# Casting the next weights between the exponential and the second table load, in the hybrid attention, RWKV-7 and PEER block

## The reference

```python
def peer_ffn(xn, peer_wq, peer_subkeys, peer_u, peer_v):
    ...
    best_s, best_pos = lax.top_k(cand_s, PEER_TOPK)
    idx = jnp.take_along_axis(cand_i, best_pos, axis=-1)
    gates = jax.nn.softmax(best_s, axis=-1)
    ...
        u_g = peer_u[ic]
        h = jax.nn.gelu(jnp.einsum('chkd,cd->chk', u_g, xc).astype(f32), approximate=False) * gc
        v_g = peer_v[ic]
        return jnp.einsum('chk,chkd->cd', h.astype(peer_v.dtype), v_g)
```

## Time and profile before

| | |
|---|---|
| Time, median of 3 runs | 948.08 us (948.0 to 948.29) |
| The profiled execution's own time | 948.34 us |
| Its span, first to last instruction | 946.3 us |
| TensorE busy, share of the span | 937.5 us, 99% |
| Chain that ended last | TensorE 98% |
| Granted TensorE clock | 0.998 |

### The profile page before, as it was taken

One profiled execution on the slowest core, in us unless ns is written; L12 is line 12 of the kernel. 1 busy time (PEld: TensorE's weight loads), 2 busy tenths in 40 slices (PEclk: granted clock), 3 DMA queues, 4 the chain that ended last, 5 costly groups with the idle time before them and its releaser, 6 DMA issues.

```text
span 946.3 us, 21227 instructions
## 1 busy us (share of the span) xinstructions
PE 937.5 (99%) x7136; PEld 903.5 (95%) x7136; DVE 756.3 (80%) x1645; ACT 623.8 (66%) x1231; POOL 645.9 (68%) x326
## 2 busy tenths in 40 slices
PE   9999999999999999999999999999999999999997
PEld 8998898898889999999999999999999999999996
DVE  7684674745755799888788888749999999999997
ACT  6874377655657567677899999865555555555554
POOL 4696635487425999999988889975655566567650
PEclk9999999999999999999999999999999999999999
DMA  7463312355654766666655556679999999999991
GB/s 268 146 235 133 134 49 94 126 183 181 223 195 137 247 218 219 219 220 212 196 184 181 183 202 225 220 262 409 409 390 390 393 388 378 403 392 377 400 356 45
DMA packets 67041, 232.32 MB, mean 246 GB/s; under 512 B 8211, under 2 KB 10259, under 8 KB 66860
## 3 DMA queue, kind: packets, MB, share of 16 engines
q1 hardware_dynamic: 52732, 180.78, 53.8%
q0 software_dynamic: 13824, 50.34, 14.0%
q10 hardware_dynamic: 432, 0.55, 0.2%
HBM read 229.67 MB, written 1.06 MB: 244 GB/s over the span
## 4 chain that ended last, share of the span: by engine, by line
PE 98%; DVE 1%; DMA 1%; ACT 0%; issue 0%; POOL 0%; DVEq 0%
PE PS L1008 21%; PE PS L1079 20%; PE PS L1012 12%; PE PS L1083 12%; PE PS L559 6%; PE PS L954 3%; PE PS L568 3%; PE PS L636 2%; PE PS L640 2%; PE PS L637 2%; PE PS L965 2%; PE PS L1033 1%; PE PS L1034 1%; PE PS L549 1%; PE PS L736 1%; PE PS L551 1%
## 5 line engine op out<-in xcount | busy, mean ns | idle before, releaser
L1649 POOL TENSOR_TENSOR lo<-raw,hi 128x1024 fp32r<-128x1024 f32 x191 | 457.6, 2416 | 130.5 <-ACT hi L1167 130.1
L1167 ACT CAST hi<-raw 128x1024 fp32r<-128x1024 f32 x202 | 211.5, 1048 | 56.3 <-DMA raw<-in_u_units 34.0
L1008 PE MATMUL PS<-xb,hi 128*128 128x416 f32 x1024 | 219.8, 356 | 0.0
L1079 PE MATMUL PS<-xb,hi 128*128 128x416 f32 x1008 | 213.2, 352 | 0.0
L1008 PEld LDWEIGHTS PS<-xb,hi 128*128 128x128 f32 x1024 | 182.6, 189 | 0.9
L1079 PEld LDWEIGHTS PS<-xb,hi 128*128 128x128 f32 x1008 | 179.2, 189 | 1.0
L2369 DVE TENSOR_TENSOR lo<-raw,hi 128x2048 fp32r<-128x2048 f32 x63 | 144.2, 2289 | 7.2 <-ACT hi L1526 7.0
L1526 ACT CAST hi<-raw 128x1024 fp32r<-128x1024 f32 x128 | 134.1, 1048 | 4.8 <-DMA raw<-in_v_units 4.8
L1012 PEld LDWEIGHTS PS<-xb,lo 128*128 128x128 f32 x1024 | 133.3, 191 | 1.8 <-POOL lo L1649 1.2
L1012 PE MATMUL PS<-xb,lo 128*128 128x208 f32 x1024 | 133.7, 273 | 0.0
L1083 PEld LDWEIGHTS PS<-xb,lo 128*128 128x128 f32 x1008 | 132.3, 191 | 1.2 <-DVE lo L2369 0.8
(11 more groups left out here) (391 smaller groups left out, 1510.5 us busy)
## 6 DMA issues: line engine op xcount, KB each, us to landing
raw<-in_u_units SPq DMA_DIRECT2D x128, 512.0 KB, 3.2
raw<-in_v_units SPq DMA_DIRECT2D x128, 512.0 KB, 6.7
raw<-in_w_in_units SPq DMA_DIRECT2D x43, 512.0 KB, 3.3
raw<-in_w_q_units SPq DMA_DIRECT2D x16, 512.0 KB, 3.4
raw<-in_w_proj_units SPq DMA_DIRECT2D x8, 512.0 KB, 3.3
raw<-in_w_out_units SPq DMA_DIRECT2D x8, 512.0 KB, 3.3
arena<-bias_rows SPq DMA_DIRECT2D x2, 512.0 KB, 5.7
arena<-in_subkeys_t SPq DMA_DIRECT2D x1, 1024.0 KB, 6.8
```

The lines of the kernel that those rows point to most:

```text
L1008: mm(o[:, 0:2 * TD], hi[:, w, P * k:P * k + P], joined[:, k, 0:2 * TD], start=(k == 0), stop=False, skip_group_check=True)
L1079: return mm(PS[:, V_BANKS[c], 0:2 * TD], hi[:, (U_V + j) % 4, P * c:P * c + P], coef_slot(u + j)[:, 0:2 * TD], start=start, stop=False, sk ...
L1167: nc.scalar.copy(hi[:, j, :], raw[:, j, :]).then_inc(hi_made, 1)
L1649: nc.gpsimd.tensor_tensor(lo[:, w, :], raw[:, w, :], hi[:, w, :].bitcast(F32), ALU.subtract).then_inc(lo_pool, 1)
```

## The change

ScalarE's rows for units 52 to 55 are put in another order. The cast for unit 56 (`hi_ahead(U_U, PICKS_AT, 2)`) stands between the exponential and the load of the gelu table, where it stood behind the right copy of unit 53. The gelu of unit 52 stands directly behind the right copy of unit 53, where it stood behind the right copy of unit 54. Nothing is added or removed.

```diff
             first_half_gelu(PICKS_AT, -1)
             act.wait_ge(shift_made, 2)
             nc.scalar.activation(bvs, bvs, ACT.Exp).then_inc(exp_made, 1)
+            hi_ahead(U_U, PICKS_AT, 2)
             nc.scalar.preload_act_table(ACT.Gelu)
             right_copy(PICKS_AT, 1)
-            for j in (2, 3):
-                hi_ahead(U_U, PICKS_AT, j)
-                right_copy(PICKS_AT, j)
-                first_half_gelu(PICKS_AT, j - 2)
+            first_half_gelu(PICKS_AT, 0)
+            right_copy(PICKS_AT, 2)
+            hi_ahead(U_U, PICKS_AT, 3)
+            right_copy(PICKS_AT, 3)
+            first_half_gelu(PICKS_AT, 1)
             with act.Fori(PICKS_AT + 1, FIRST // 4) as i:
```

## The result

The changed kernel takes 950.95 us (median of 20 runs, 948.08 to 955.94), the kernel before 948.68 us (20 runs, 947.45 to 951.27). The ratio is 1.0026 with a 95% interval from 1.0016 to 1.0035: 1.5 to 3.3 us slower. I had forecast 0.26 us less, and a range that ended at 948.6.

The account below looks back on a forecast made before the run. TensorE, with 98% of the chain that ended last, was taken as the bound. One term, −0.26 us, took the profiled 948.34 to 948.08; the median's 0.26 us lower level gave 947.82 us, range 947.3 to 948.6.

Parts of the forecast that it names:

- the one on the gelu of unit 52: ScalarE around the softmax: gelu runs 427.12 to 427.48 against 427.10 to 427.46 before, freeing unit 56's bank in time.
- the table load's move: ScalarE behind unit 56's cast: load ends at 426.76, right copy of unit 53 starts 1.08 us later, no net cost.
- a rule on table loads: Trainium skill's drain of about 1380 ns per ScalarE table switch; by it the sum was about 949.0 us.
- the gain: TensorE at unit 56's low products: wait for GpSimd's subtraction gone, 0.26 us saved, bounds 0.22 and 0.33.
- The cast starts at once: ScalarE, unit 56: cast at 424.41, right behind the exponential, 1.52 us earlier, weights landed 0.8 us ahead.
- the subtraction is ready for TensorE: GpSimd, unit 56: subtraction runs 425.54 to 427.93, wanted at 429.18, 1.2 us to spare.
- the cast of unit 57 is no bound: ScalarE, unit 57: cast 0.24 us later, subtraction done at 431.10, wanted at 431.60, half a microsecond of cover.
- The rival of the dearer table switch: ScalarE: table load waits for the cast to leave the engine, up to +0.83 us, 948.9 us; chance 0.05.
- The rival of the late weights: ScalarE: unit 56's weights land late, delaying cast, load and gelu of unit 52; up to +1.07 us, 949.15; chance 0.06.
- The rival of a gain that is lost again: TensorE: 0.26 us lost again at unit 57 or the next wait, L1083; 948.08 us; chance 0.17.

Follow-up runs that it names:

- the gelu alone: Kernel before with only the gelu of unit 52 moved ahead of the right copy of unit 54: 948.87 us, ratio 1.0002.
- the staging edit on before: Kernel before with row numbers staged ahead of the exponential, one operand in PSUM, and gates by a product with reciprocal sums in PSUM: 948.46 us, ratio 1.0005.
- both rows out of the way: Changed kernel with row numbers staged ahead of the exponential, one operand in PSUM, and gates by a product with reciprocal sums in PSUM: 948.3 us, ratio 1.0.

## Why the prediction was wrong

**The step that failed** is the one on the gelu of unit 52: "In the new order the gelu has only the copy of unit 53 ahead of it, and runs from about 427.12 to 427.48", and, of the table load's move, "Cost nothing; cover that small." I took VectorE's sum of unit 52 to start at 426.69 as before, because no VectorE row had moved. But what runs beside those rows had: my own sum moved a GpSimd subtraction to 425.54, on top of VectorE rows that had stood in GpSimd's idle time. The sum started at 428.43, and the gelu ran from 428.83. I looked at which engine waits for which semaphore, and this wait has none; it shows as the duration of a row.

The Trainium skill has the rule, on the page "SBUF — State Buffer", section "Who interferes with whom": a VectorE instruction with two inputs in SBUF contends with a GpSimd instruction that reads SBUF, copies can enter a mode that contends as well, and the one that issues second blocks until the first ends. The traces agree: 2.30, 2.44 and 2.37 us for the two-operand row against 0.29, 2.03 to 2.41 us for the copy against 0.22, and 0.29 with one operand in PSUM. In all of these GpSimd came first; no run here shows it waiting for VectorE. I had weighed a rule on table loads and missed the one that decided.

**The term that was mis-sized** is the gain: "I take the middle one, 0.26". The wait of 0.33 us for unit 56's subtraction was that one execution's. In two other profiles with the cast in its old place (the gelu alone, the staging edit on before) it is 0.07 and 0.06 us, and the chain has the low products of unit 56 at the usual 0.88 us there, so the term measures nothing. In the profile of before, unit 55's cast stood 5.76 us ahead of the transposes (421.37 to 427.13), in these two 6.01 and 6.03: the softmax and the cast behind it happened to be late by a quarter of a microsecond. Such a small wait can stand elsewhere, too: the kernel with both rows out of the way has one of 0.34 us ahead of unit 52's low products. That kernel is 0.36 us better than the profile of before in the stretch and not to be told from it in the runs.

**The range** stood on the spread of 0.3 us in three runs. Over 20 runs the kernel before goes from 947.45 to 951.27 us, and its median, 948.68, lies above the end of my range with no change at all; less 0.26 it would have been 948.42, near the end. So even a right sum would have been inside only just.

**What was right.** The cast starts at once, its weights having landed; the subtraction is ready for TensorE with time to spare; the cast of unit 57 is no bound. The rival of the dearer table switch falls: the load follows the cast after 0.02 us (424.06 + 1.03 = 425.09, 425.11), lasts 1.28 us, and the copy starts 0.01 us behind it. The drain that the Trainium skill adds to each switch (the page "ScalarE: Activation LUTs", section "What ACT_TABLE_LOAD costs") is not to be seen there either. The rival of the late weights falls too: no wait for a load stands ahead of that cast. Both rivals had the place right, the bank of unit 52, and prices, 1.07 and 0.83 us, near the 1.2 us that the stretch of the first profile grew by. That is luck, for neither had the mechanism, and neither allowed for more. The rival of a gain that is lost again did not come true either, for there was no gain; but the kernel with the gelu alone shows the like, at the gate product.

**The size.** The stretch grew by 1.2 and 1.6 us in the two profiles of the changed kernel. TensorE's lower clock adds to some executions: in the 20 runs, the 16 at 0.998 or 0.999 have a mean of 950.73 us, the 4 below a mean of 953.45, so the four lift the mean by about 0.5 us. Together that is 1.7 to 2.1 us of the 2.43 us between the means of the two lists of 20 runs. That the lower clock follows the stall is seen in the profiles of two other kernels with a longer stall; neither profile of the changed kernel fell on such an execution. What makes up the last few tenths stays open; the interval of the ratio allows for none as well. One candidate is the landing of unit 55's weights, with which the chain to the gelu of unit 52 begins: in the one profile in which it took 1.2 us longer, TensorE waited 1.0 us longer. How often it does, no run here shows.

## What to carry to other kernels

When an engine is given work earlier, look at what ran beside its idle time: VectorE rows with two SBUF operands, and copies within SBUF, can stand for the whole of a GpSimd instruction that reads SBUF, with no semaphore to show it. So read the duration of a row that did not move as well as its place, and keep one operand in PSUM, or start GpSimd behind such rows. And a wait of a few tenths in one profile is no term for a sum until a second profile has it.

## What the hardware showed that I had not expected

A stall of TensorE may cost more than itself. At waits from 1.28 to 1.86 us ahead of unit 56 the profiled executions kept a clock of 1.00; at 2.50 and 2.90 us both fell to 0.50 a little behind the restart, for about 3 us. In the first profile of the changed kernel a wait of 1.48 us lengthened the stretch by 1.2; by that measure 2.50 and 2.90 us would be 2.2 and 2.6, and it grew by 3.7 and 4.5, of which 0.2 in the second is a longer wait at the first gate product (0.35 us, not 0.12). That leaves 1.5 and 1.7 us for the clock. The rows of the windows agree: 3 us at 0.50 are 1.5 us lost. The mean clock of all executions points the same way: 0.997 or less in 0 of 87 with the order of before, 7 of 32 with the change, 3 of 5 with the stall made longer.
